# A hybrid encoder layer on one core: finer first loads, an earlier weight ring, a later overflow table, and 8-partition transfers at the end

## What is computed

```
h = x + W_out[ groupnorm( mLSTM | HGRN2 | Fourier | 2-D neighbourhood attention ) ](rmsnorm(x) @ w_in)
h = h + softmax(q k^T) v @ wo          # cross attention to 256 memory rows, 4 heads of 512
h = h + MoE(rmsnorm(h))                # 32 experts, top 2 inside the best of 4 groups
out = rmsnorm(h)

MoE, per expert e:  (silu(X_e @ w1[e]) * (X_e @ w3[e])) @ w2[e]     # w1, w3: 2048 x 512, w2: 512 x 2048
```

## Time and profile before

| | |
|---|---|
| median of the timed executions | 1819.96 us |
| the profiled execution, whole | 1820.34 us |
| its span (first to last instruction) | 1818.0 us |
| TensorE busy | 1560.7 us (86%) |
| VectorE busy | 802.6 us (44%) |
| ScalarE busy | 490.8 us (27%) |
| DMA bytes moved | 561.27 MB, mean 309 GB/s |

### The profile page before, as it was taken

One profiled execution on the slowest core, in us unless ns is written; L12 is line 12 of the kernel. 1 busy time (PEld: TensorE's weight loads), 2 busy tenths in 40 slices (PEclk: granted clock), 3 DMA queues, 4 the chain that ended last, 5 costly groups with the idle time before them and its releaser, 6 DMA issues.

```text
span 1818.0 us, 25956 instructions
## 1 busy us (share of the span) xinstructions
PE 1560.7 (86%) x11206; PEld 999.5 (55%) x11206; DVE 802.6 (44%) x1103; ACT 490.8 (27%) x698; POOL 41.5 (2%) x25
## 2 busy tenths in 40 slices
PE   7999999999999999999797668767777868886785
PEld 7899899899777889988432213222222222221221
DVE  5665655798576554344442322323222323232233
ACT  5454444644355344244400000000000000000002
POOL 0000000032000000000000000000000000000001
PEclk9999999999999999999998986987878777687877
DMA  8755545444355565438999999999999999999995
GB/s 328 261 190 171 181 151 184 151 149 154 128 185 185 185 189 170 163 114 330 386 420 430 428 433 428 431 431 429 432 428 429 429 432 431 430 430 432 429 426 238
DMA packets 96492, 561.27 MB, mean 309 GB/s; under 512 B 8705, under 2 KB 8961, under 8 KB 78209
## 3 DMA queue, kind: packets, MB, share of 16 engines
q1 hardware_dynamic: 95232, 557.56, 76.9%
q10 hardware_dynamic: 1152, 2.10, 0.3%
HBM read 557.54 MB, written 2.10 MB: 308 GB/s over the span
## 4 chain that ended last, share of the span: by engine, by line
PE 59%; DMA 35%; DVE 4%; ACT 1%; issue 1%; SPq 0%; DVEq 0%; ACTq 0%
DMA arena<-in_moe_w_dram 35%; PE ps L652 7%; PE ps L658 7%; PE ps L653 7%; PE ps L654 7%; PE ps L659 6%; PE ps L660 6%; PE ps L1049 4%; PE ps L1077 4%; PE ps L1092 3%; DVE arena L2289 1%; PE ps L1061 1%; PE ps L1017 1%; PE ps L878 1%; PE ps L897 1%; PE ps L798 1%
## 5 line engine op out<-in xcount | busy, mean ns | idle before, releaser
L1049 PE MATMUL ps<-arena 128*32 128x512 f32 x1840 | 292.9, 751 | 163.7 <-DMA arena<-in_moe_w_dram 160.5
L1663 DVE TENSOR_TENSOR w_lo<-arena,w_hi 128x1024 fp32r<-128x1024 f32 x264 | 318.3, 1247 | 236.5 <-ACT w_hi L1219 236.3
L2289 DVE SCALAR_TENSOR_TENSOR arena<-ps,arena 128x1024 f32<-128x1024 f32 x128 | 164.2, 1284 | 427.3 <-PE ps L1092 427.2
L1219 ACT ACTIVATE w_hi<-arena 128x1024 fp32r<-128x1024 f32 x264 | 264.8, 1052 | 300.0 <-PE ps L654 160.8
L1049 PEld LDWEIGHTS ps<-arena 128*32 128x32 f32 x1840 | 55.0, 122 | 315.7 <-issue 285.4
L1525 ACT ACTIVATE arena<-ps 128x512 f32<-128x512 f32 x64 | 38.2, 597 | 594.2 <-PE ps L1049 594.2
L652 PE MATMUL ps<-x_hi,w_hi 128*128 128x256 f32 x512 | 146.6, 286 | 12.0 <-DVE w_lo L1663 12.0
L1077 PE MATMUL ps<-arena 128*32 128x512 f32 x928 | 130.1, 707 | 24.8 <-DMA arena<-in_moe_w_dram 24.8
L653 PE MATMUL ps<-x_lo,w_hi 128*128 128x256 f32 x512 | 145.8, 285 | 0.0
L654 PE MATMUL ps<-x_hi,w_lo 128*128 128x256 f32 x512 | 145.7, 285 | 0.0
L1092 PEld LDWEIGHTS ps<-d_hi,pick 32*128 32x128 f32 x256 | 29.5, 230 | 182.7 <-DVE arena L2289 137.3
(11 more groups left out here) (342 smaller groups left out, 2521.3 us busy)
## 6 DMA issues: line engine op xcount, KB each, us to landing
arena<-in_moe_w_dram SPq DMA_DIRECT2D x66, 4096.0 KB, 42.4
arena<-in_moe_w_dram SPq DMA_DIRECT2D x36, 2048.0 KB, 37.5
arena<-in_w_in_dram SPq DMA_DIRECT2D x52, 1024.0 KB, 5.1
extra<-in_moe_w_dram SPq DMA_DIRECT2D x19, 2048.0 KB, 40.1
arena<-in_xa_wk_dram SPq DMA_DIRECT2D x16, 1024.0 KB, 5.0
arena<-in_xa_wv_dram SPq DMA_DIRECT2D x16, 1024.0 KB, 5.0
arena<-in_w_out_dram SPq DMA_DIRECT2D x16, 1024.0 KB, 5.0
arena<-in_xa_wq_dram SPq DMA_DIRECT2D x16, 1024.0 KB, 5.0
```

The source lines that it names most:

```text
L1049: last = mm(ps[EB * c:EB * (c + 1), m, :], xe[par][:, ECH * i + c, :], piece(n, m, i)[:, c, :], start=(i == 0), stop=(i == ECH - 1))
L1219: fn(hi_ring[(2 * n + u) % 4][:], ring_a[i][:, 2 * u:2 * u + 2, :], ACT.Copy).then_inc(S["w_hi"], 1)
L1663: V.tensor_tensor(w_lo[i][:, 2 * u:2 * u + 2, :], ring_a[i][:, 2 * u:2 * u + 2, :], hi_ring[(2 * n + u) % 4][:].bitcast(F32), ALU.subtract ...
L2289: V.scalar_tensor_tensor(hv, flat(ps[:, b0:b0 + 2, :]), weight_of(e, j), hv, ALU.mult, ALU.add).then_inc(S["c_add"], 1)
```

## The change

- First loads: x_t comes in four transfers (k-tiles 0-1, 2-3, 4-7, 8-15) where it had two, and chunk 0 of the weights in two halves. Signals of the x_t split are given every two k-tiles. ScalarE issues one small activation (`one_act`) before its first wait. TensorE issues 16 matmuls (`WARM`) on a constant tile before group 0.
- Ring: unit 2 is issued after group G_WQ + 1, unit 5 before the wait on `xs_o`, units 0, 1, 3 and 7 between the chunks of G_XO + 1. Units 8, 4, 6 and 9 come in halves, each when its buffer is free.
- Overflow table: VectorE computes it after block 4 instead of before block 0; the matmul is ahead of TensorE's block 7 instead of block 1; the copy to the table follows VectorE's block 5. VectorE's loop starts at block 7 instead of 3.
- Last two w2 halves: each is 16 transfers of 8 partitions (64 KB) where it was one of 128 partitions (1 MB).

```diff
+OV_AT = 7
...
+WARM = 16
+LANES = 8
...
+        one_act = arena(201, 1)
...
-                loads[k] += 2 if at in IN_PARTS or at in (6, 9) else 1
+                loads[k] += P // LANES if at == len(order) - 1 else 2 if at in IN_PARTS or at in (4, 6, 8, 9) else 1
...
-            sp.dma_start(x_t[:, 0:CH, :], ins["x_t"][:, 0:CH, :]).then_inc(S["xt_in0"], 16)
-            load_dense(0, (0,))
-            sp.dma_start(x_t[:, CH:, :], ins["x_t"][:, CH:, :]).then_inc(S["xt_in1"], 16)
-            load_dense(0, (1, 2, 3))
+            first = dense_chunk(0, 0)
+            sp.dma_start(x_t[:, 0:2, :], ins["x_t"][:, 0:2, :]).then_inc(S["xt_in0"], 16)
+            sp.dma_start(ring_a[0][:, 0:2, :], first[:, 0:2, :]).then_inc(S["w_first"], 16)
+            sp.dma_start(x_t[:, 2:CH, :], ins["x_t"][:, 2:CH, :]).then_inc(S["xt_in1"], 16)
+            sp.dma_start(ring_a[0][:, 2:CH, :], first[:, 2:CH, :]).then_inc(s_ring[0], 16)
+            sp.dma_start(x_t[:, CH:2 * CH, :], ins["x_t"][:, CH:2 * CH, :]).then_inc(S["xt_in2"], 16)
+            load_dense(0, (1,))
+            sp.dma_start(x_t[:, 2 * CH:, :], ins["x_t"][:, 2 * CH:, :]).then_inc(S["xt_in3"], 16)
+            load_dense(0, (2, 3))
...
-            sp.wait_ge(S["x_lo"], NCH)
+            sp.wait_ge(S["x_lo"], KT // 2)
...
-            for g in range(G_WQ + 1, G_XO + 2):
+            load_dense(G_WQ + 1)
+            load_unit(2)
+            for g in range(G_WQ + 2, G_XO + 1):
                 load_dense(g)
-            load_unit(2)
+            load_unit(5)
             sp.wait_ge(S["xs_o"], XA_H)
+            for i, at in enumerate((0, 1, 3, 7)):
+                load_unit(at)
+                load_dense(G_XO + 1, (i,))
             load_dense(G_XO + 2)
-            for at in (0, 1):
-                load_unit(at)
-            load_dense(G_XO + 3, (0, 1))
-            load_unit(3)
-            load_dense(G_XO + 3, (2, 3))
-            for at in (5, 7):
-                load_unit(at)
+            load_dense(G_XO + 3)
+            sp.wait_ge(S["chunk_used"], (G_XO + 3) * NCH + 1)
+            half_unit(8, 0)
             sp.wait_ge(S["chunk_used"], (G_XO + 3) * NCH + 2)
-            load_unit(8)
+            half_unit(8, 1)
+            half_unit(4, 0)
             sp.wait_ge(S["chunk_used"], (G_XO + 3) * NCH + 3)
             half_unit(6, 0)
             half_unit(9, 0)
             sp.wait_ge(S["chunk_used"], (G_XO + 4) * NCH)
-            load_unit(4)
+            half_unit(4, 1)
             half_unit(6, 1)
             half_unit(9, 1)
...
-                    sp.dma_start(piece(NE - 1, 2, 2), expert_rows(NE - 1, 2, 2, 1)).then_inc(S["dn_last"], 16)
-                    sp.dma_start(piece(NE - 1, 2, 3), expert_rows(NE - 1, 2, 3, 1)).then_inc(s_slot[at % len(slot_kib)], 16)
+                    for i, landed_ in ((2, S["dn_last"]), (3, s_slot[at % len(slot_kib)])):
+                        for p0 in range(0, P, LANES):
+                            sp.dma_start(piece(NE - 1, 2, i)[p0:p0 + LANES], expert_rows(NE - 1, 2, i, 1)[p0:p0 + LANES]).then_inc(landed_, 16)
...
                         if c % 2 == 0:
+                            if g == 0:
+                                pe.wait_ge(S["x_lo"], k // 2 + 1)
                             pe.wait_ge(S["w_lo"], half + 1)
...
-            for i in range(NCH):
-                pe.wait_ge(S["x_lo"], i + 1)
-                dense_split(0, W_IN[0][1], split[G_IN], part=[i])
+            pe.wait_ge(S["pool_step"], 1)
+            for _ in range(WARM):
+                mm(ps[:, 7, 0:P], one_pp, one_pp, start=True, stop=True)
+            dense_split(0, W_IN[0][1], split[G_IN])
...
                 if isinstance(n, int) and n == NE - 1 and i == 2:
-                    pe.wait_ge(S["dn_last"], 16)
+                    pe.wait_ge(S["dn_last"], 16 * (P // LANES))
...
+                if isinstance(n, int) and n == OV_AT - 1 and q == 0:
+                    pe.wait_ge(S["tab_dve"], 1)
                 if not (isinstance(n, int) and 4 * n + q <= behind):
                     pe.wait_ge(S["c_add"], n * 4 + (q - behind))
...
                 if counts:
                     pe.wait_ge(S["r_dve"], 4)
+                    pe.wait_ge(S["c_add"], 4 * back)
                     mm(ps[:, 7, 0:2 * OVB], ones, flat(ov_rhs), start=True, stop=True).then_inc(S["r_pe"], 1)
...
-                block_n(n, n - 1, n % 2, counts=(n == 1))
+                block_n(n, n - 1, n % 2, counts=(n == OV_AT))
...
-                    if k % CH == CH - 1:
+                    if k % 2 == 1:
                         last.then_inc(S[done], 1)
...
+            def first_high(u):
+
+                fn(w_hi[0][u][:], ring_a[0][:, 2 * u:2 * u + 2, :], ACT.Copy).then_inc(S["w_hi"], 1)
+
+            act.wait_ge(S["pool_step"], 1)
+            fn(one_act, one_pp[:, 0:1], ACT.Copy)
             act.wait_ge(S["front_in"], 16)
             act.wait_ge(S["xt_in0"], 16)
-            by_gain(x_t, split[G_IN][0], 0, range(CH), "x_hi")
-            high(0, (0,))
+            by_gain(x_t, split[G_IN][0], 0, range(2), "x_hi")
+            act.wait_ge(S["w_first"], 16)
+            first_high(0)
             act.wait_ge(S["xt_in1"], 16)
+            by_gain(x_t, split[G_IN][0], 0, range(2, CH), "x_hi")
+            act.wait_ge(s_ring[0], 16)
+            first_high(1)
+            act.wait_ge(S["xt_in2"], 16)
             by_gain(x_t, split[G_IN][0], 0, range(CH, 2 * CH), "x_hi")
             high(0, (1,))
+            act.wait_ge(S["xt_in3"], 16)
             by_gain(x_t, split[G_IN][0], 0, range(2 * CH, KT), "x_hi")
             high(0, (2, 3))
...
-            by_gain_low(x_t, split[G_IN], 0, range(CH), "x_hi", "x_lo")
-            low(0, (0,))
+            by_gain_low(x_t, split[G_IN], 0, range(2), "x_hi", "x_lo")
+            low(0, (0,), (0,))
+            by_gain_low(x_t, split[G_IN], 0, range(2, CH), "x_hi", "x_lo")
+            low(0, (0,), (1,))
...
+            def over_blocks():
+
+                one32 = ones[:, 0:NE]
+                step(V.tensor_scalar(blocks, count, float(EB), None, ALU.is_gt))
+                for k in range(2, OVK + 1):
+                    step(V.tensor_scalar(rtmp, count, float(k * EB), None, ALU.is_gt))
+                    step(V.tensor_tensor(blocks, blocks, rtmp, ALU.add))
...
+                last.then_inc(S["r_dve"], 1)
+
+            def over_table():
+
+                dve.wait_ge(S["r_pe"], 3)
+                ov = ps[:, 7, 0:2 * OVB]
+                V.tensor_copy(table[0:1, 32:32 + OVB], ov[0:1, 0:OVB])
+                V.tensor_copy(table[0:1, 96:97], blk_in[0:1, NE - 1:NE])
+                V.tensor_copy(over_first, ov[:, OVB:2 * OVB]).then_inc(S["tab_dve"], 1)
+                dve.wait_ge(S["tab_dve"], 1)
+
+            for n in range(7):
                 block_n(n, n % 2)
-            with dve.Fori(0, NE // 2 - 3) as e:
-                block_n(e * 2 + 3, 1)
-                block_n(e * 2 + 4, 0)
+                if n == 4:
+                    over_blocks()
+                if n == OV_AT - 2:
+                    over_table()
+            with dve.Fori(0, NE // 2 - 5) as e:
+                block_n(e * 2 + 7, 1)
```

More of the change, by code:

```diff
@@ L379, in program @@
         S = {}
-        for n in ["xt_in0", "xt_in1", "x0_in", "x_in", "mem_in", "mem_t_in", "front_in", "cmix_in", "cdft_in", "cmask_in", "wg_in",
+        for n in ["xt_in0", "xt_in1", "xt_in2", "xt_in3", "w_first", "x0_in", "x_in", "mem_in", "mem_t_in", "front_in", "cmix_in", "cdft_in", "cmask_in", "wg_in",
                   "bias_in0", "bias_in1", "wr_in", "fgain_in", "out_done",
@@ L1655, in turned_lo, with low @@
                     last.then_inc(S["ts_lo"], 1)
-            def low(g, part):
+            def low(g, part, halves_=range(2)):
                 for i in part:
                     n, hi_ring = split_chunk(g, i)
-                    for u in range(2):
+                    for u in halves_:
                         dve.wait_ge(S["w_hi"], 2 * n + u + 1)
@@ L1691, in by_gain_low @@
                 for k in part:
-                    if k % CH == 0:
-                        dve.wait_ge(S[waits], k // CH + 1)
+                    if k % 2 == 0:
+                        dve.wait_ge(S[waits], k // 2 + 1)
                     last = V.scalar_tensor_tensor(lo[:, k, :], src[:, k, :], cols[:, gain * KT + k:gain * KT + k + 1],
                                                   hi[:, k, :].bitcast(F32), ALU.mult, ALU.subtract)
-                    if k % CH == CH - 1:
+                    if k % 2 == 1:
                         last.then_inc(S[done], 1)
@@ L2245, in _ @@
             tokens(1, 1)
[L2247 to L2264, removed]
             def gating(n):
@@ L2336, in finish_n @@
                 inverse(1)
[L2338 to L2344, removed]
-                block_n(n, n % 2)
-            with dve.Fori(0, NE // 2 - 3) as e:
-                block_n(e * 2 + 3, 1)
-                block_n(e * 2 + 4, 0)
+            def over_blocks():
[4 more added lines that the diff above has]
```

(17 more changed lines are left out.)

## The result

The median went from 1819.96 to 1828.33 us (five runs each, 1826.43 to 1829.36 after). The ratio of the runs is 1.0033, with a 95% interval of 1.0020 to 1.0046: slower, by 6.0 us (3.6 to 8.4). The two medians are 8.4 us apart. The forecast was 1819.0, in a range that ended at 1821.5. The profiled execution after took 1828.46 us, its span 1826.4: 8.4 more than the span before.

What follows compares the result with a forecast made beforehand. TensorE was taken to bound the dense stage, the weight stream at 430 GB/s the expert stage. Gains 3.0 + 0 + 1.3 less 3.3 made 1.0 us off 1820.34: forecast median 1819.0 us, its own range 1816.5 to 1821.5, overall 1812.0 to 1821.5.

Steps and rivals of the forecast that it cites:

- the last two pieces: End of the expert stage: eight engines, some trailing, carry the 2.10 MB; 3.3 us later, bounds -2.1 and +4.9.
- First loads: Start of the dense stage: first matmul at 8.8 us, 2.5 earlier; with faster first matmuls 3.0 us gained, bounds 1.2 and 4.4.
- The slow first matmuls: First matmuls, 11.35 to 16 us: the 16 new matmuls ahead give back between 0 and 1.9 us, taken as 0.5.
- Ring filled earlier: Before the experts: six units issued in spare DMA time; gain 0, bounds 0 and 1.8 us.
- the 900 us window: Start of expert 0, 900 to 905 us at 275 GB/s: 1.8 us lost, to stay as weak despite a fuller ring.
- Overflow table: Start of expert 0: without TensorE's 3.63 us wait an issue comes 4 us earlier; gain 1.3 us, bounds 0.5 and 1.7.
- The issues: SyncE's 32 issues for the last pieces: 0.33 to 0.43 us each, 12 us, over at 1769, still behind a full queue.
- Rival 4: Last pieces: each small transfer holds its engines longer than its bytes; at 0.6 us each about 1828 us; chance 0.07.
- Rival 1: Last pieces: the eight engines are the leading ones, so the end comes 2.1 us earlier; 1813.6 us; chance 0.30.

Runs made afterwards that it cites:

- u: Kernel without computation: sixteen transfers, all into partitions 0 to 7, no units ahead; 18.2 us at 55 GB/s.
- l: Kernel without computation: behind three 2 MB units, 32 transfers of 8 partitions in steps of four, only to partitions below 64; 26.1 us.
- a: Kernel without computation, the control: behind three 2 MB units, 2 transfers of 128 rows of 8 KB; 22.1 us in the second such kernel.
- s: Kernel without computation: behind three 2 MB units, 32 transfers of 8 partitions in steps of four; 25.5 us.
- y: Kernel without computation: behind three 2 MB units, 16 transfers of 16 partitions in steps of four; 24.9 us.
- w: Kernel without computation: 32 transfers of 8 partitions in steps of four, no units ahead; 21.6 us.
- b: Kernels without computation: behind three 2 MB units, 32 transfers of 8 neighbouring partitions; 33.6 us in the first such kernel, 27.8 in the second.

## Why the prediction was wrong

**The step that failed** is that of the last two pieces, "2.4 to 4.9 us later than now", of which I took 3.3. Its frame was right: eight rows occupy eight engines, and the set holds trailing ones. That no row of the kernel before shows, it was my assumption; the trace after has eight 4 byte increments a transfer, and two engines carry its last rows (51 GB/s). Two terms were wrong.
- *A missing mechanism.* The estimate moved 2.10 MB "on eight at 213", with each packet as long as ever. In truth the small transfers' 8 KB packets took 0.47 to 0.57 us from 1781 to 1790 us, against 0.31 with large transfers (and 1.20 in u, 55 to 58 GB/s for eight engines), and the trailing engines' units were slowed as well, their 16 KB packets taking 0.93 to 1.19 us and not 0.61. The last packet of a unit ended at 1791.25 us with large transfers and at 1795.21 in the changed kernel: 4.0 us.
- *A term taken at its middle.* The trailing engines of the set then had 32 rows of 8 KB instead of 16, and took their whole share after all others were done. From the last unit packet to the last row it was 10.25 us (1805.46) instead of 4.93 (1796.18): 5.3 more, just over my upper bound of 4.9. The 6 us at 51 GB/s are two such engines.

Sum 9.3, against the 3.3 that I took. The last down, started that much later, was also slower, 1.94 us against 1.07 with large transfers (PEclk is 0.50 at 1804 to 1808 us, and 0.88 at 1796 to 1800 with large transfers): 10.2, which is the distance of the spans (1826.4 and 1816.2) and of the ratios.

**First loads**, forecast 3.0 (2.5 + 0.5): 2.0 by the ratio (0.4 to 3.6). The first matmul came 2.5 us earlier, as worked out. The slow first matmuls, taken at 0.5, ran 0.12 us apart at once, 1.7 in the first group; that the idle behind the 16 takes part of it back, for which I took so little, no run shows, and after 2.4 us of idle it took nothing; how much of that reaches the end is open, as said above. Expert 0 starts 3.9 and 3.6 us earlier (894.31 and 894.69 in the kernels with steps of four and with sixteen rows, 898.25 before), and only 2.1 in the changed kernel. The difference of 1.8 is mostly a stretch of 3.4 us at half clock that only the changed kernel's execution had of these three, below.

**Ring filled earlier**, forecast 0: 0, by two comparisons. I was right in the number and wrong in saying that the 900 us window would stay weak: it became full, and the one before it nearly empty, so that the 30 us as a whole moved no more (376 and 380 GB/s).

**Overflow table**, forecast 1.3 (0.5 to 1.7): 1.6 in the profile, 0.9 by the ratio. The wait went, and the issue came 5.9 us earlier relative to expert 0 (13.4 us behind its first matmul and not 19.3), where I had said 4: 4.6 are the earlier start of the downs, and 1.3 the first two downs, 2.0 us long and not 3.3. Over these 30 us PEclk was 1.00 after and 0.89 before, which I had not counted.

**The issues** were to be over at 1769; SyncE was held until 1784.6, 1.02 us an issue. By themselves behind units 32 issues took 11.2 us. Why it was held here was not tried; that it costs nothing is argued only, from the trailing engines reaching these rows ten microseconds later.

**Rival 4** had the total (1828) with a chance of 0.07, but by luck, for its mechanism is refuted: size and number of transfers are not what costs. Transfers of 64 KB had 8 KB packets of 0.31 us in l, and 128 rows of 2 KB cost 0.7 us. Rival 1 (the small transfers even out the lag) was given 0.30: of the eight engines two trailed (51 GB/s for 6 us), so it did not hold here. Whether another set of engines would even out the lag was not tried.

## What to carry to other kernels

Before you cut a transfer, ask not only how many engines can carry it but into which partitions they write at one time: here 8 KB packets took 0.31 us in transfers of all 128 partitions, and 1.20 us in sixteen transfers into the same eight neighbours, 55 GB/s together. Read DMA share and GB/s as one number, rate over 16 times the share: here a busy engine moved 27 GB/s by itself and 14 to 14.5 in the tails with transfers of eight and sixteen neighbouring rows. And when an uneven tail is handed to fewer engines, price it at the whole share behind the slowest of them.

## What the runs showed of the hardware

- How long a DMA packet takes depended on the partitions written at one time: 8 KB packets took 0.31 us in transfers to 128 partitions (a) and to eight in steps of four (l, s), 0.60 to sixteen in steps of four (y), and 1.20 to the same eight neighbours again and again (u).
- An issue with steps of four partitions held SyncE's queue 0.67 us (w), one of neighbouring partitions 0.35 (b).
- TensorE's granted clock fell to 0.50 of full speed for 3.4 to 6.8 us between 176 and 189 us in some executions. The windows of PEclk in the kernel without the fill, then in the one with steps of four, whose dense stage is the same in these operations:

```profile
176.00:180.00 4.00, 4.00 (x14) 2.88 (x14) 2.60 (x3) 2.19 (x3) 0.00 (x0) 0.77 1.04 388
180.00:184.00 4.00, 4.00 (x16) 3.17 (x15) 3.38 (x6) 0.47 (x2) 0.00 (x0) 0.80 0.33 121
```
```profile
176.00:180.00 4.00, 4.00 (x18) 2.94 (x19) 2.61 (x3) 2.26 (x3) 0.00 (x0) 1.00 1.04 385
180.00:184.00 4.00, 4.00 (x20) 3.28 (x19) 3.73 (x6) 0.42 (x2) 0.00 (x0) 1.00 0.39 141
```

TensorE was busy for all 8 us of these windows in both. The stretch was in 6 of 8 profiled executions with the finer loads and in 1 of 4 with the old ones, so one execution's start of expert 0 can be up to 3.6 us off (897.91 with steps of sixteen, which had it, against 894.31 with steps of four, which had not); why it falls, and whether the head start makes it likelier stays open.
- The first matmuls after an idle start were 0.21 us apart for 4.6 us while PEclk read 1.00, and 0.12 with 16 matmuls ahead of them, even after 2.4 us of idle. That column does not show this slow start: the trace's list of granted clocks begins only at 15.88 us there and at 14.74 in the kernel without the 16 matmuls, just where the spacing changes (15.94 and 14.76), and a window ahead of its first entry reads 1.00.
